# Prompt attention: query tiles dealt into two sets of equal causal work, rows longest first, the last two one key tile later

## The reference: what is computed

```python
s = (jnp.einsum('bqhr,bkr->bhqk', qlb, c_kv)
     + jnp.einsum('bqhp,bkp->bhqk', qrb, k_r)).astype(jnp.float32)
s = jnp.where(kpos[None, :] <= qpos[:, None], s, -jnp.inf)
p = jax.nn.softmax(s, axis=-1).astype(c_kv.dtype)
return jnp.einsum('bhqk,bkr->bqhr', p, c_kv)
```

## Time and profile before

| what | value |
|---|---|
| median of 3 runs | 1586.86 us (1586.74 to 1593.02) |
| the profiled execution's own time | 1591.77 us |
| its span, first to last instruction | 1590.1 us |
| PE busy over the span | 1481.4 us (93%) |
| DVE, ACT, POOL busy over the span | 644.6, 343.5, 476.6 us |
| mean granted TensorE clock | 0.962 of full speed |

### The profile page before, as it was taken

The page is one execution under the profiler, slowest core; times in us unless marked ns, Lnnn a source line. Parts: engine busy times, 40 slices in busy tenths (PEclk is TensorE's granted clock), DMA queues, the critical chain, the costliest instruction groups (busy, mean ns, idle before and its releaser), DMA issues.

```text
span 1590.1 us, 21965 instructions
## 1 busy us (share of the span) xinstructions
PE 1481.4 (93%) x8472; PEld 1355.3 (85%) x8472; DVE 644.6 (41%) x1186; ACT 343.5 (22%) x692; POOL 476.6 (30%) x353
## 2 busy tenths in 40 slices
PE   6989996899998888899899999999999999999996
PEld 4757896788787453799799999999999999999995
DVE  4792036566765231411732324142332324141426
ACT  3312122555564210310410000101010000001022
POOL 1251223342433000045662332332331331331313
PEclk9989998999998988799999999999999999999998
DMA  6020101000011544041120110110111111111003
GB/s 215 1 84 14 41 17 48 17 17 1 28 54 43 155 134 120 1 179 40 40 93 27 54 50 29 53 48 32 53 44 35 53 41 38 53 40 40 27 1 113
DMA packets 39762, 86.33 MB, mean 54 GB/s; under 512 B 6258, under 2 KB 18290, under 8 KB 38994
## 3 DMA queue, kind: packets, MB, share of 16 engines
q1 hardware_dynamic: 39698, 85.48, 16.8%
HBM read 79.62 MB, written 5.84 MB: 54 GB/s over the span
## 4 chain that ended last, share of the span: by engine, by line
PE 75%; DVE 10%; issue 5%; SPq 4%; ACT 3%; POOL 2%; DMA 1%; DVEq 0%; POOLq 0%; ACTq 0%
PE ps L646 23%; PE ps L648 22%; PE ps L647 22%; PE ps L869 2%; PE ps L654 1%; PE ps L935 1%; DMA x<-in_x 1%; SPq L385 1%; SPq L381 1%; SPq L384 1%; PE ps L976 1%; DVE x L1405 1%; SPq L374 1%; POOL h2L L622 1%; DVE mx L1628 1%
## 5 line engine op out<-in xcount | busy, mean ns | idle before, releaser
L1790 DVE TENSOR_TENSOR av<-st,ps 128x384 f32<-128x384 f32 (+1 forms) x66 | 35.2, 533 | 393.1 <-ACT st L1375 393.1
L646 PE MATMUL ps<-acH,dnH 128*128 128x384 f32 (+1 forms) x528 | 173.8, 329 | 4.4 <-DVE x L1802 4.4
L1802 DVE TENSOR_TENSOR x<-x,ps 128x384 f32<-128x384 f32 (+1 forms) x264 | 137.2, 529 | 92.5 <-PE ps L648 92.2
L648 PE MATMUL ps<-acH,dnL 128*128 128x384 f32 (+1 forms) x528 | 172.2, 326 | 0.0
L646 PE MATMUL ps<-h2H,upH 128*128 128x384 f32 (+1 forms) x528 | 172.1, 326 | 0.0
L647 PE MATMUL ps<-acL,dnH 128*128 128x384 f32 (+1 forms) x528 | 172.1, 326 | 0.0
L648 PE MATMUL ps<-h2H,upL 128*128 128x384 f32 (+1 forms) x528 | 172.0, 326 | 0.0
L647 PE MATMUL ps<-h2L,upH 128*128 128x384 f32 (+1 forms) x528 | 172.0, 326 | 0.0
L1375 ACT ACTIVATE st<-ps 128x384 f32<-128x384 f32 (+1 forms) x66 | 31.3, 474 | 644.9 <-PE ps L648 644.9
L646 PEld LDWEIGHTS ps<-acH,dnH 128*128 128x128 f32 x528 | 99.1, 188 | 7.8 <-DVE x L1802 7.6
L647 PEld LDWEIGHTS ps<-acL,dnH 128*128 128x128 f32 x528 | 99.1, 188 | 0.3
(11 more groups left out here) (264 smaller groups left out, 3382.1 us busy)
## 6 DMA issues: line engine op xcount, KB each, us to landing
raw<-in_w_ff SPq DMA_DIRECT2D x66, 512.0 KB, 3.4
cp<-in_cache SPq DMA_DIRECT2D x64, 256.0 KB, 2.6
x<-in_x SPq DMA_DIRECT2D x4, 1088.0 KB, 7.9
raw<-in_w_out SPq DMA_DIRECT2D x8, 512.0 KB, 3.7
raw<-in_w_in SPq DMA_DIRECT2D x6, 512.0 KB, 3.6
out_y<-x SPq DMA_DIRECT2D x4, 768.0 KB, 3.6
raw<-in_w_v SPq DMA_DIRECT2D x4, 512.0 KB, 4.1
raw<-in_w_u SPq DMA_DIRECT2D x4, 512.0 KB, 3.5
```

Source lines behind the costliest of these rows:

```text
L646: nc.tensor.matmul(out, wh, xh, start=start, stop=False)
L648: return nc.tensor.matmul(out, wl, xh, start=False, stop=stop)
L1790: nc.vector.tensor_tensor(a, st[:, q % 2, 0:n], ps[:, 2 * (q % 2) + 1, 0:n], ALU.mult).then_inc(f_act, 1)
L1802: nc.vector.tensor_tensor(x, x, ps[:, 4 + r % 4, 0:n], ALU.add).then_inc(y_free, 1)
```

## The change

The query tiles of a head are dealt anew: even units take tiles 2, 3, 4, 5 (18 tiles of work, 6 key tiles), odd units tiles 0, 1, 6, 7 (18 tiles, 8 key tiles). Inside a unit the rows are made with the longest first, so row 3, which DVE multiplies, is now the shortest (128 columns in odd units, 384 in even ones). The rows of the next unit stand at key tiles 0, 1, 3 and 4 instead of 0 to 3; where u%4 = 3 they stay at 4 to 7. Two units have 14 turns and products instead of 12. `move_weighed` stores two pieces of 256 columns.

```diff
 def tr_count(u):
-    return 12 * (u // 2) + 4 * (u % 2)
+    return 14 * (u // 2) + 6 * (u % 2)
...
 def row_at(u, kt):
-    qi = kt - (4 if u % 4 == 3 else 0)
-    return qi if u + 1 < UNITS and 0 <= qi < 4 else None
+    at = (4, 5, 6, 7) if u % 4 == 3 else (0, 1, 3, 4)
+    return at.index(kt) if u + 1 < UNITS and kt in at else None
...
+QSETS = ((2, 3, 4, 5), (0, 1, 6, 7))
+
+def row_tile(u, i):
+    return QSETS[u % 2][3 - i]
+
+def key_tiles(u):
+    return QSETS[u % 2][3] + 1
+
+def first_place(u, kt):
+    return sum(qt < kt for qt in QSETS[u % 2])
...
             def weigh(u):
-                blk = u % 2
-                nk = 4 * (blk + 1)
+                nk = key_tiles(u)
...
-                    for qi in range(max(0, kt - 4 * blk), 4):
+                    for qi in range(4 - first_place(u, kt)):
...
-                        at = prob_at(4 * blk + qi) + P * kt
-                        last = nc.tensor.transpose(ps[:, 4 + x % 2, P * qi:P * qi + P], prob[:, at:at + P],
+                        at, col = prob_at(row_tile(u, qi)) + P * kt, P * (3 - qi)
+                        last = nc.tensor.transpose(ps[:, 4 + x % 2, col:col + P], prob[:, at:at + P],
...
             def move_turned(u):
-                blk = u % 2
-                for kt in range(4 * (blk + 1)):
+                nk = key_tiles(u)
+                for kt in range(nk):
...
-                    if qi == 3:
-                        invert(4 * (u + 1) + qi)
+                    if kt and row_at(u, kt - 1) == 3 or qi == 3 and kt == nk - 1:
+                        invert(4 * (u + 1) + 3)
```

More of the change, by code:

```diff
@@ L549, in normalise @@
                 for qi in range(3):
-                    r, qt = 4 * u + qi, 4 * (u % 2) + qi
+                    r, qt = 4 * u + qi, row_tile(u, qi)
                     n = P * (qt + 1)
@@ L839, in score @@
                     pe.wait_ge(made_r, 2)
-                r, qt = 4 * u + qi, 4 * blk + qi
+                r = 4 * u + qi
                 if r >= 2:
@@ L874, in product @@
                     x = tr_count(u) + kt
-                    c0 = P * max(0, kt - 4 * blk)
+                    c0 = P * first_place(u, kt)
                     pe.wait_ge(t_free, x + 1)
@@ L1256, in move_weighed @@
             def move_weighed(u):
-                p, hh, blk = u // 4, u // 2 % 2, u % 2
+                p, hh = u // 4, u // 2 % 2
                 act.wait_ge(pv_x, tr_count(u + 1))
                 part = slice(VH * hh, VH * hh + VH)
-                hi(aT[part, p, 512 * blk:512 * blk + 512], ps[part, 6 + u % 2, :]).then_inc(o_free, 1)
+                quarters = aT[part, p, 0:SEQ].rearrange("p (a n) -> p a n", a=4)
+                mine = quarters[:, 0:4:3, :] if u % 2 else quarters[:, 1:3, :]
+                hi(mine, ps[part, 6 + u % 2, :].rearrange("p (a n) -> p a n", a=2)).then_inc(o_free, 1)
             def move_turned(u):
-                blk = u % 2
-                for kt in range(4 * (blk + 1)):
+                for kt in range(key_tiles(u)):
                     x = tr_count(u) + kt
-                    c0 = P * max(0, kt - 4 * blk)
+                    c0 = P * first_place(u, kt)
                     act.wait_ge(t_ready, x + 1)
@@ L1618, in invert @@
                 if qi == 3:
-                    qt = 4 * (u % 2) + 3
+                    qt = row_tile(u, qi)
                     row = prob[:, prob_at(qt):prob_at(qt + 1)]
@@ L1633, in move_turned @@
             def move_turned(u):
-                blk = u % 2
-                for kt in range(4 * (blk + 1)):
+                nk = key_tiles(u)
+                for kt in range(nk):
                     x = tr_count(u) + kt
-                    c0 = P * max(0, kt - 4 * blk)
+                    c0 = P * first_place(u, kt)
                     qi = row_at(u, kt)
-                    if qi is not None and kt < 4 * blk + 3 and not row_late(u, kt):
+                    if qi is not None and kt < nk - 1 and not row_late(u, kt):
                         maximum(u + 1, qi)
@@ L1647, in move_turned @@
                         move_gen(u // 4 + 1, i)
-                    if qi is not None and (kt == 4 * blk + 3 or row_late(u, kt)):
+                    if qi is not None and (kt == nk - 1 or row_late(u, kt)):
                         maximum(u + 1, qi)
-                    if qi == 3:
-                        invert(4 * (u + 1) + qi)
+                    if kt and row_at(u, kt - 1) == 3 or qi == 3 and kt == nk - 1:
+                        invert(4 * (u + 1) + 3)
             for i in range(GEN):
```

4 lines of the change are left out of this document (2 added, 2 removed).

## The result

The changed kernel takes 1598.51 us (median of 13 runs, 1593.09 to 1604.93), beside 1589.83 us for the kernel before (13 runs, 1586.50 to 1593.21). The ratio is 1.0056, with a 95% interval from 1.0045 to 1.0068: slower by a little over the half per cent that a measurement here can tell. The prediction's 1589 was too low by 9.5 us, inside its range of 1574 to 1600. The profiled execution took 1596.81 us, its span is 1595.0 us (1590.1 before). One single execution of all that follow, in experiment 6, ran in a much slower state (2422 us) and is left out.

What follows compares the result with a forecast made beforehand. PE was taken to set the pace. Units 1 to 13 at 194.8 against 194.2 us, unit 0 +2.2, unit 13's split +1.5 and last unit -2.1 gave +2.4 on 1586.9: about 1589 us, range 1574 to 1600.

Steps and rivals of the forecast that it cites:

- The large wait: Start of units 1, 5, 9, 13: PE's waits for DVE's multiplication of row 3, 9.1 us in all, would go.
- the rival of a falling clock: Units: small waits start about eight 1.2 GHz stretches of 1.3 us, +10 us, 1600 in all; chance 0.12.
- Small waits: At the turns: many PE waits of 0.2 to 1.2 us come; transposes' waits for pTL grow to about 10 us.
- behind it on ACT stand the store aT and only then the copy of key tile 2: Even unit, behind the second exponential: store 0.59 us, then copy 0.60, ending at 7.4; PE waits some 0.8 us.
- Unit lengths: Even units 10.8 us, odd 11.3, u%4 = 3 28.25; units 1 to 13 together 194.8 against 194.2 before.
- PE's work is unchanged within 0.1 us for a pair of units.: Even plus odd unit: transposes, score columns and product columns equal in sum, with two more triples of products.
- Of which PE works about 8.9: Even unit: PE works about 8.9 us of the forecast 10.8 us.
- the small waits don't come: Even units take 9.2 us, odd 10.3: -17 us, so 1572, or 1581 with half of it; chance 0.24.
- Filling the pipe and unit 0: Start of attention: filling the pipe before unit 0 unchanged, unit 0 itself +2.2 us like other even units.
- Unit 13 and the split, +1.5: Unit 13: DVE's last multiplication can meet POOL's output-weight split, between 0 and 2.7 us, taken as 1.5.
- The rival of POOL holding DVE in every unit: Each unit's last multiplication waits for POOL's row 2: +7 us, 1596 or more with splits at full price; chance 0.10.
- Last unit, -2.1: Last unit, 16.94 us with the sample matmuls: 8 tiles less of transposes and products, some 0.26 us each, -2.1 us.

Runs made afterwards that it cites:

- experiment 6: Changed kernel with the next unit's rows at key tiles 0 to 3 instead of 0, 1, 3 and 4: 1593.51 us, ratio 1.0019.
- experiment 7: Changed kernel with its dealing and row places kept, but the rows shortest first: 1606.48 us, ratio 1.0105.
- experiment 12: Kernel of experiment 4 with DVE's maximum of row 2 behind pTL of key tile 3 (u%4 other than 3): 1598.69 us, ratio 1.0057.
- experiment 4: Changed kernel with ACT's store of the unit before behind the copy of key tile 2 instead of ahead of it: 1589.55 us, ratio 1.0007.
- experiment 8: Kernel before, with its dealing and row places kept and only the rows made longest first: 1584.35 us, ratio 0.9960.
- experiment 3: Changed kernel with POOL's splits of two output weights in units 11 and 12 instead of 12 and 13: 1593.80 us, ratio 1.0023.
- experiment 11: Kernel of experiment 8 with sample 0's rotary parts and sample 1's page numbers ahead of SP's waits, and the store behind key tile 2's copy: 1590.23 us, 0.9998.
- experiment 1: Changed kernel with SP fetching sample 0's rotary parts ahead of the wait for the split and the load of ukT: 1592.25 us, ratio 1.0008.

## Why the prediction came out as it did

**The large wait goes.** Right. It was to be near 0 outside unit 13, and is not in the list at all.

**The clock in the units.** Right: 1.00 in each of units 1 to 13 shown, instead of 0.88 and 0.90 in two of them. PE's waits of under 1 us started no half-clock stretch there, so the rival of a falling clock didn't come in this kernel's units. It isn't empty, though: experiment 7 has one such stretch in unit 1 and experiment 12 one in unit 13.

**Small waits.** Right in size by the profile's list: about 10 us of transposes waiting for pTL were forecast, 9.1 came, and 2.1 of products; for u%4 = 3 a score's wait of 1.2, and it is 0.83:

```profile
402.28 0.47 PE L664 MATMUL ps<-kH,qH 128*128 128x512 f32 x1 [0.83 <-ACT prob L1268]
```

In the even unit the step "behind it on ACT stand the store aT and only then the copy of key tile 2" is what happened, and experiment 4 showed it as a cause.

**Unit lengths.** Even 10.8 forecast, 10.59 to 10.87 measured; odd 11.3, measured 11.11 to 11.72; u%4 = 3 28.25, measured 27.80; units 1 to 13 194.8, measured 193.23.

**"PE's work is unchanged within 0.1 us for a pair of units."** By the busy column it looks wrong. Units 5 and 6 have PE busy 20.14 us now; unit 9 and an even unit at full clock made 10.71 and 8.32, 19.03. "Of which PE works about 8.9" is 10.0 in the even unit. The groups by form (xcount | busy us, mean ns | idle before), first after, then before, seem to show that a 256-column product doesn't cost half of one of 512:

```profile
L664 PE MATMUL ps<-pTH,hvH 128*128 128x256 f32 x48 | 18.0, 374 | 1.4 <-DVE pTL L1662 1.3
L664 PE MATMUL ps<-pTH,hvH 128*128 128x512 f32 x32 | 15.6, 487 | 0.0
```

```profile
L646 PE MATMUL ps<-pTH,hvH 128*128 128x256 f32 x16 | 4.5, 280 | 0.0
L646 PE MATMUL ps<-pTH,hvH 128*128 128x512 f32 x48 | 23.7, 495 | 0.0
```

From start to start at full clock, less listed waits, the 18 matmuls of 256-column products in units 5 and 6 of experiment 4 take 3.29 us and the 12 of 512 columns 3.21. In experiment 8 it is 6 in 0.70 and 18 in 4.69. The same columns are booked with 1.1 us more in a pair of units. One part is that the first product behind transposes holds PE some 0.09 us longer, at either width (0.32 against 0.23 us at 512 columns); here it is in experiment 4 at 256, 0.21 us, and the next 0.11:

```profile
370.15 0.38 PE L886 MATMUL ps<-ident,prob 128*128 128x128 f32 x2
370.29 0.36 PE L664 MATMUL ps<-pTH,hvH 128*128 128x256 f32 x1
370.50 0.28 PE L665 MATMUL ps<-pTL,hvH 128*128 128x256 f32 x1
370.61 0.29 PE L666 MATMUL ps<-pTH,hvL 128*128 128x256 f32 x1
```

The larger part is waiting that PE's rows don't list. The waits of the weight loads (PEld) in units 1 to 13 show it, in experiment 4:

```profile
PEld ps L886 <- DVE pTL L1662: 10.6, 36, 0.8
PEld ps L664 <- DVE pTL L1662: 6.0, 19, 1.0
```

and in experiment 8:

```profile
PEld ps L886 <- DVE pTL L1661: 2.2, 1, 2.2
```

So in experiment 4 55 weight loads were held up until a pTL was done. In experiment 8 that happens once; there the load stands ahead of its matmul (376.48 and 376.66 us for a 256-column product), while in experiment 4 the same product's load and matmul both start at 383.55. Such a late load, and the tail of the matmul before it, count as busy. An estimate: give every matmul of units 1 to 13 the time from start to start that its kind takes in experiment 8 (a 256-column product behind transposes, which is not found there, its own); that sums to 174.7 us for the new dealing and 174.4 for the old. So, short of waits, the prediction's step nearly holds, and PE's 180 us of the busy column hold some 5 us of hidden waiting. By the same estimate an even unit is 9.3 to 9.4 us of work, not 8.9 and not 10.0. The forecast of 10.8 came out by the chain of dependences that the prediction gave, of which experiment 4 took one link away. The rival "the small waits don't come", with 9.2 us for an even unit, is not excluded by PE's work; experiment 4 goes a part of that way, to 10.1.

**Filling the pipe and unit 0.** "No change" for the pipe was wrong: from the first score to unit 0's transposes it is 9.41 us instead of 7.08, because the long rows come first. Cut as the other units are, at its first score, unit 0 starts 1.1 us later, and grew by 2.1 (11.46 instead of 9.35), where 2.2 was forecast. Together +3.2 against +2.2.

**Unit 13 and the split, +1.5.** DVE's multiplication of 384 columns met POOL's split and took 1.04 us; where it meets nothing it is 0.42:

```profile
492.46 1.04 DVE L1640 TENSOR_SCALAR prob<-prob,rsm 128x384 f32<-128x384 f32 x1
```

PE didn't wait for it, but for the pTL queued behind it on DVE: a product waits 0.79 us there (at 493.88), and 0.17 in experiment 3, where nothing meets this multiplication. Unit 13 is 11.72 us, and 11.11 in experiment 3: the split costs 0.6 us, and the term was 0.9 us too large. The rival of POOL holding DVE in every unit is seen in 0.48 us for 128 columns, where experiment 6 has 0.29, and PE has no listed wait for it. The exclusion of the two engines that the Trainium skill (SBUF — State Buffer, "Who interferes with whom") describes is borne out by 1.04 here and 2.72 in experiment 11. That whoever issues first has the ports isn't: in experiment 11 DVE's row starts 0.03 us ahead of POOL's and is the one that takes long.

**Last unit, -2.1.** 15.07 against 16.94: -1.9.

**The step that failed** is the one that isn't in the text. The sum came to +2.4 (its terms as printed make 2.3) and the attention measures +0.3 in its span; the other stages were taken as unchanged, and they hold the loss. POOL's time was followed to its effect on DVE and PE ("it splits output weights behind the rows"), and not to who else waits for the split: SP's queue, with the pages of all samples behind it. By the ratio the change costs 8.9 us (0.56%); 2.4 were forecast, 6.5 are missing, and experiment 1 prices SP's chain at 7.6, give or take 3. (The other 3 us by which 1589 is too low are the base: the kernel before was at 1586.86 in three runs and is at 1589.83 in thirteen.) The 2.6 us in the output projection are partly a half-clock stretch at 685 us and partly the first load of x, for which DVE waits 6.34 us instead of 5.04 before:

```profile
683.41 1.88 DVE L1760 TENSOR_TENSOR x<-x,ps 128x384 f32<-128x384 f32 x4 [6.34 <-DMA x<-in_x]
```

Every kernel with the new dealing had 5.9 to 6.5 us there, every one with the old dealing 5.0 to 5.1. Why stays open; nothing was tried on it.

That 1598.5 lies inside the range is luck in part: it is in the stretch over 1595 that was given 0.22, and what was to lead there, a falling clock or POOL holding DVE in every unit, is not what did.

**In sum.** Longest first gives 0.40% (experiment 8). The new dealing takes 0.59% of that kernel's time back (experiment 6) and the later rows 0.37%, 0.96% in all. Two edits give that back: 0.48% by SP's order, 0.49% by the store's place and what follows from it. With both mended (0.9957) it is level with the simple version (0.9960). Equal sets gain nothing beyond the order of rows: the large waits are paid for with many small ones, of which the profile lists only a part.

## What to carry to other kernels

A step that moves an engine's work later moves everything that waits for that engine: follow each semaphore it raises to the queues of SP too, and see what is queued behind the wait there. When work is dealt out anew in pieces of other widths, take each kind of piece from start to start where nothing waits, and don't take busy time for work: look at the waits of the weight loads too. And when rows change places, look at every queue for an instruction that nobody waits for (here a store) standing ahead of one that somebody does. Try the parts of a compound change one by one: here one part gave 0.4%, and the others took 0.96%.

## What the runs showed of the hardware that was not expected

- SP needs long for a sample's fetches: from the first rotary issue of one sample to the pages of the next 13.1 us after (500.89 to 513.98) and 12.6 before, with 16 issues in about 8 us and about 5 us to read page numbers.
- A matmul of 256 columns at the head of a product took 374 ns in the mean after, against 280 before; start to start it holds PE 0.21 us behind transposes, and 0.22 behind another product when its weight load was released late by pTL, against 0.12 where the load stood ahead (experiments 4 and 8). The profile books both as busy.
- The length of one wait doesn't tell whether a half-clock stretch begins. In the units before, three stretches stood at or shortly behind waits of 1.72, 1.75 and 3.66 us, and none at one of 1.74; experiment 8 has none at 1.76. After, none stood in units 1 to 13, with waits of up to 0.8 us, but one began during a wait of 1.22 us, the second over 1.2, while the pipe filled (289.5 us), and in experiment 7 one began behind waits of no more than 0.6.
